# A conditioned decoder layer with expert retrieval on one core: eight first weight tiles under way, modulation rows on GpSimd's queue, top-k over two phases, gathers of u and v by turns

## The chip, the cores and the metric

One NeuronCore of a Trainium2 chip runs the whole kernel as one program. The metric is the device time of one execution in microseconds (us). The engines work in parallel, each through its own instruction list: PE (TensorE, matmul), DVE (VectorE), ACT (ScalarE), POOL (GpSimd) and SP (SyncE, which here only issues transfers). They wait for each other through semaphores. Transfers run on 16 DMA engines whoever issues them.

## The reference, cut to what matters

A prompt of 1024 tokens and 8 decoding streams of 4 tokens (32 tokens, "sample") go through one layer. All data are float32, the model width D is 1024.

```python
mod = silu(c) @ w_ada + b_ada                 # 6 rows: sh1, sc1, gt1, sh2, sc2, gt2
h1 = rmsnorm(x, g_norm1) * (1 + sc1) + sh1
mix = token_mixer(h1, ...)                    # w_in, causal pooling, conv of width 31, LayerNorm, w_out
x = x + gt1 * mix
h2 = rmsnorm(x, g_norm2) * (1 + sc2) + sh2
# PEER: 8 heads, 128 x 128 = 16384 experts, 16 chosen per head: 128 experts for each token
s = (h2 @ w_query) . sub_keys                 # two score rows of 128 for each head
sv, si = top_k(s, 16); fv, fpos = top_k(sums of the 16 x 16 pairs, 16); gate = softmax(fv)
a = u_table[eid] . h2;  act = gelu(a) * gate;  out = sum over the 128 experts of act * v_table[eid]
y = rmsnorm(x + gt2 * out, g_final)
```

Each token so reads 128 rows of 4 KB from `u_table` and 128 from `v_table`: some 1.1 GB in all.

## The kernel before, in words

**Blocks and phases.** The tokens are 8 blocks of 128 (b = 0..7) and the sample block SB = 8. Retrieval runs in phases p = 0..8 of 32 slots each. In slot c of phase p the kernel gathers u rows for block p and v rows for block p-1, four gathers each (CH = 4); one gather is an indirect DMA, issued by POOL, which brings 128 rows of 4 KB (512 KB). Phase 0 has only u, phase 8 only v and the sample block. The gathers land in two rings of six places each (`u_ring`, `v_ring`). `u_fetch` waits until DVE has freed the place six gathers back, `v_fetch` until PE has. POOL runs both in one instruction list, so whatever it waits for holds all gathers behind it.

**DVE in a slot** (`chunk`, L1324): four dots, one for each u gather (multiply by h2, sum over 1024 elements), and then the steps that `lay_out` has put into the slot before (DVE_LAG = 1). **PE in a slot** (`tokens`, L1687): the weighted sum of the v rows, and then the steps of the slot.

**Steps.** `lay_out` writes the order by hand-set costs. `fill` lays the mixer and the queries of the block groups [2,3,4] and [5,6,7,SB] from slot `at` on. `spread` lays the top-k pieces: each block has 4 parts (two heads each), each part 6 pieces (`piece`, i = 0..5), and behind them `exp` (the softmax's exponential on ACT), `nrm` (its normalisation on DVE, which waits for ACT's `exp`) and, once for a block, `turn` (the transposed expert numbers for the v gathers). The u gathers of part q of block b, at slot 32b + 8q, wait for that part's numbers. ACT runs the steps in slot order too, with a gelu after every eighth chunk, which waits for DVE's dots of that chunk.

**The head.** Before phase 0 the kernel computes the modulation (`modulation(n)`, n = 0..11, each from two tiles of `w_ada` of 1 MB; PE, then DVE adds the bias, L1089), then the mixer of blocks 0 and 1 (`project` L1509, `convolve` L1526, `taps` L1177, `pool_out`, `mean` L1556, `variance`, `mix` L1579 and L1581) and their queries and scores (L1605, L1621; ACT copies the scores out at L912). Weight tiles come through four places of 1 MB (`places`, PLACE = i % 4): tile i is issued on SP's queue once tile i-4 is used. SP also stores the modulation results to DRAM (`mod_store`), reads them back as rows broadcast to all 128 partitions (`mod_row` L535, for gt1, S2 and A2) and loads the output bias (`bout_load` L571), all in line with the tiles. The convolution's first PE_CONV channel groups run on PE with diagonal matrices that ACT makes (L819), the others as 31 taps on DVE. At the end DVE does the six pieces of part 0 of block 0, and the phases begin. After the last tile of the head SP loads x of blocks 2 and 3 (`xr_load`, L567), which DVE's step `xn` waits for.

## Time and profile before

| | |
|---|---|
| time, median of 3 runs | 3471.78 us (3471.12 to 3472.04) |
| the profiled execution | 3469.63 us, its span 3467.7 us |
| mean granted clock of TensorE | 0.82 of full speed |
| instructions in the profile | 30586 |
| busy: PE, DVE, ACT, POOL | 64%, 61%, 10%, 66% of the span |
| moved by DMA | 1253.56 MB, mean 361 GB/s |

Times below are counted from the start of the span. A row of instructions gives start and duration; in square brackets stands how long its engine was idle before it, and which instruction or transfer ended that. "issue" is time in which nothing that the profile shows was waited for. Several instructions of one kind in a row are merged and counted (x60). The phases of the retrieval begin with a dot of DVE: phase 0 at 238 us, phase 1 at 628, then 1023, 1383, 1800, 2164, 2506, 2847 and 3189.

### The profile page before, as it was taken

Reading aid. Unit: us, or ns where it says so; the run is one execution under the profiler, and the core shown is the slowest. Engines: PE = TensorE matmul, PEld = TensorE weight load, DVE = VectorE, ACT = ScalarE, POOL = GpSimd, SP = SyncE. Lnnn points to the kernel's source line nnn. Section 1 sums busy time; section 2 is a strip of 40 time slices with the busy share of each in tenths; the row PEclk is TensorE's granted clock in tenths of the full one; section 3 lists DMA queues with packets and bytes.
Section 4 is the critical chain, followed back from the end, with each engine's and each line's share of the span. In section 5 each row is a group of like instructions: output and inputs, shape, how many; then the busy total and the mean of one; then the engine's idle time right before and its main releaser. Section 6 shows DMA issues by size and latency. Waiting matters only on the chain.

```text
span 3467.7 us, 30586 instructions
## 1 busy us (share of the span) xinstructions
PE 2206.3 (64%) x9781; PEld 976.0 (28%) x9781; DVE 2125.2 (61%) x4835; ACT 360.6 (10%) x778; POOL 2283.7 (66%) x2213
## 2 busy tenths in 40 slices
PE   7873895467847899656448777454445444454576
PEld 6563452135512355211114444111111111111111
DVE  2345888645686677675655666667766776776301
ACT  3101141000111022100000010000000000000000
POOL 0012545676777777777757777777777777777675
PEclk9996897689978999888768999767777777776799
DMA  7666756899999999999989999999999999999998
GB/s 238 187 234 212 274 194 242 324 403 405 407 385 403 407 398 406 361 402 398 370 289 404 407 408 408 390 409 406 402 393 406 401 406 394 403 407 374 382 392 330
DMA packets 377968, 1253.56 MB, mean 361 GB/s; under 512 B 38056, under 2 KB 46912, under 8 KB 377793
## 3 DMA queue, kind: packets, MB, share of 16 engines
q0 software_dynamic: 304128, 1107.43, 82.3%
q1 hardware_dynamic: 51505, 100.14, 8.6%
q10 hardware_dynamic: 22176, 44.04, 3.4%
q8 instruction: 78, 1.28, 0.2%
q14 instruction: 81, 0.66, 0.0%
HBM read 1230.01 MB, written 22.06 MB: 361 GB/s over the span
## 4 chain that ended last, share of the span: by engine, by line
POOL 29%; DMA 27%; PE 24%; issue 10%; DVE 5%; SPq 3%; ACT 1%; DVEq 1%; POOLq 0%; ACTq 0%
DMA v_ring<-in_v_table_dram,eidt 21%; POOL u_ring L772 14%; POOL v_ring L789 13%; PE bank L1687 11%; PE bank L1526 4%; PE bank L1509 3%; SPq L535 2%; PE bank L1605 2%; DMA u_ring<-in_u_table_dram,eid 2%; DVE u_ring L1324 2%; DMA u_ring<-in_v_table_dram,eidt 1%; POOL u_ring L789 1%; DMA wring<-in_w_ada_dram 1%; PE bank L1581 1%; PE bank L1466 0%
## 5 line engine op out<-in xcount | busy, mean ns | idle before, releaser
L1687 PE MATMUL bank<-v_ring,act_x 128*32 128x512 f32 x3984 | 1184.2, 809 | 960.5 <-DMA v_ring<-in_v_table_dram,eidt 950.8
L1324 DVE CUSTOM_DVE_ANT_0 u_ring<-u_ring,h 128x1024 f32<-128x1024 f32 x1056 | 1281.8, 1226 | 785.4 <-DMA u_ring<-in_u_table_dram,eid 715.1
L772 POOL DMA_INDIRECT u_ring<-in_u_table_dram,eid x1024 | 1149.7, 1123 | 728.6 <-issue 299.8
L789 POOL DMA_INDIRECT v_ring<-in_v_table_dram,eidt x996 | 1036.0, 1040 | 396.4 <-issue 239.5
L1687 PEld LDWEIGHTS bank<-v_ring,act_x 128*32 128x32 f32 x3984 | 271.0, 135 | 1797.2 <-issue 1781.8
L1605 PE MATMUL bank<-hbuf,wring 128*128 128x128 f32 (+1 forms) x2048 | 243.8, 279 | 3.4 <-DMA wring<-in_w_query_dram 3.4
L1605 PEld LDWEIGHTS bank<-hbuf,wring 128*128 128x128 f32 x2048 | 236.4, 194 | 32.1 <-issue 28.4
L1526 PE MATMUL bank<-zc,dring 128*128 128x384 f32 (+1 forms) x512 | 194.4, 507 | 9.3 <-ACT dring L819 9.3
L1509 PE MATMUL bank<-hbuf,wring 128*128 128x384 f32 (+2 forms) x512 | 165.8, 483 | 23.4 <-ACT hbuf L832 22.5
L1509 PEld LDWEIGHTS bank<-hbuf,wring 128*128 128x128 f32 x512 | 99.0, 196 | 91.6 <-issue 64.0
L1581 PE MATMUL bank<-wring,mixt 128*128 128x512 f32 (+1 forms) x256 | 121.9, 627 | 0.0
L1347 DVE TENSOR_TENSOR scratch<-bank,mod 128x512 f32<-128x512 f32 x18 | 11.6, 687 | 179.2 <-PE bank L1687 177.9
L1526 PEld LDWEIGHTS bank<-zc,dring 128*128 128x128 f32 x512 | 87.8, 192 | 58.0 <-issue 26.1
L819 ACT ACTIVATE dring<-ident,cw 128x128 f32<-128x128 f32 x256 | 81.3, 393 | 123.5 <-PE bank L1528 88.2
L927 ACT ACTIVATE dot<-dot 128x32 f32<-128x32 f32 x33 | 7.6, 231 | 809.8 <-DVE dot L1324 788.2
L1324 DVE DVE_READ_ACCUMULATOR2_ANT dot<- 128x1 f32 x1056 | 87.5, 83 | 0.0
L1687 PE MATMUL bank<-u_ring,act_x 128*32 128x512 f32 x240 | 59.2, 611 | 22.5 <-DMA u_ring<-in_v_table_dram,eidt 22.5
L789 POOL DMA_INDIRECT u_ring<-in_v_table_dram,eidt x60 | 56.4, 940 | 21.7 <-issue 16.1
L1581 PEld LDWEIGHTS bank<-wring,mixt 128*128 128x128 f32 (+1 forms) x256 | 46.6, 189 | 74.9 <-issue 74.8
L902 ACT ACTIVATE qt<-bank 128x512 f32<-128x512 f32 (+1 forms) x36 | 20.2, 562 | 378.3 <-PE bank L1605 378.3
L1528 PEld LDWEIGHTS bank<-zcs,dring 128*128 128x128 f32 x248 | 46.9, 189 | 33.1
L1250 DVE TENSOR_TENSOR work<-fhalff,iota 128x512 f32<-128x512 f32 x72 | 49.8, 692 | 8.0 <-issue 0.9
(217 smaller groups left out, 1613.5 us busy)
## 6 DMA issues: line engine op xcount, KB each, us to landing
u_ring<-in_u_table_dram,eid POOLq DMA_INDIRECT x1024, 7.4
wring<-in_w_out_dram ACTq DMA_DIRECT2D x16, 1024.0 KB, 11.9
wring<-in_w_query_dram ACTq DMA_DIRECT2D x16, 1024.0 KB, 12.2
v_ring<-in_v_table_dram,eidt POOLq DMA_INDIRECT x996, 7.7
wring<-in_w_ada_dram SPq DMA_DIRECT2D x12, 1024.0 KB, 10.5
v_ring<-in_w_ada_dram SPq DMA_DIRECT2D x12, 1024.0 KB, 6.7
wring<-in_w_in_dram ACTq DMA_DIRECT2D x10, 1024.0 KB, 11.6
xr<-in_x_prompt_dram SPq DMA_DIRECT2D x16, 512.0 KB, 7.7
```

Of the source, the lines that this page charges most:

```text
L535: sp.dma_start(out.rearrange("p (n j c) -> p n j c", n=2, j=4), src.unsqueeze(0).broadcast_to([count, 2, 4, P])).then_inc(ready, 16)
L772: pool.indirect_dma_start(u_ring[:, n % NU], None, u_table[0], bass.IndirectOffsetOnAxis(ap=col, axis=0)).then_inc(u_in[n % NU], 16)
L789: pool.indirect_dma_start(place, None, v_table[0], bass.IndirectOffsetOnAxis(ap=eidt[:, b % RING, t:t + 1], axis=0)).then_inc(landed, 16)
L819: last = act.activation(diag_at(g, c, j), ident[:, :], ACT.Copy, scale=cw[:, j, c:c + 1])
L1250: dve.tensor_tensor(hot[:, :, :, :], fhalff[:, :, a * K:(a + 1) * K].unsqueeze(3).broadcast_to(shape), iota[:, :].unsqueeze(1).unsqueeze(1 ...
L1324: dve.tensor_tensor_reduce(u_ring[:, n % NU], u_ring[:, n % NU], h2[:, b % 2], 1.0, 0.0, ALU.mult, ALU.add, dot[:, b % 2, k:k + 1]).then_i ...
L1509: last = pe.matmul(ps[PROJ[c]][:, 0:n], w[:, k, c * P:(c + 1) * P], h1t[:, h * HK + k, 0:n], start=(h + k == 0), stop=(h * HK + k == KC - 1))
L1526: last = pe.matmul(ps[2 + c % 2][:, 0:np], diag_at(g, c, j), zc[:, c, j:j + np], start=(j == 0), stop=(j == CK - 1))
L1528: last = pe.matmul(ps[7][:, c * S:(c + 1) * S], diag_at(g, c, j), zcs[:, c, :, j:j + TS], start=(j == 0), stop=(j == CK - 1))
L1581: last = pe.matmul(bank, mixt[:, h * HK + k, t0:t0 + n], w[:, k, :], start=False, stop=(h * HK + k == KC - 1))
L1605: last = pe.matmul(q_bank(b)[:, a * n:(a + 1) * n], w[:, k, a * P:(a + 1) * P], h2_cols(b)[:, h * HK + k, :], start=(h + a + k == 0), stop ...
L1687: last = pe.matmul(acc[h][j * S:(j + 1) * S, :], act_x[:, i % 2, j, a:a + S], v_place(n)[0][:, h * HALF:(h + 1) * HALF], start=(c == 0), s ...
```

## The change

It has five parts.

1. **First tiles.** Tiles 0 to 7 get eight places of their own (three in `u_ring`, one more in `v_ring`); from tile 8 on four places are used as before. The load of the sub-keys, which shares memory with tile 7, waits for all eight (`mod_ps` 8). ACT makes its first eight diagonals after x's columns instead of before them.
2. **Modulation rows.** The stores of modulation results 4 to 9, the broadcast rows of gt1, S2 and A2 and the first load of the output bias are issued by POOL, which waits for each result in turn; 10 and 11 stay on SP. Semaphores of the sample's rows are separate now. PE and DVE do modulations 4 to 9 in one run behind the convolution (PE), and behind taps and boxes (DVE); PE's `pool_out` comes after them.
3. **Convolution split.** PE_CONV goes from 2 to 1: one channel group on PE, three as taps on DVE.
4. **Steps.** `exp` and `nrm` of part 0 of block 0 move from slot 0 to slot 5, the mixer of the second group begins at slot 5 instead of 2, block 0's parts 1 to 3 are spread over slots 0 to 18, and block b's four parts over slots 18 + 30(b-1) to 18 + 30b (block 1 was within slots 13 to 31, block b from 8 slots after its predecessor's phase began to 5 slots after its end).
5. **Gathers.** POOL issues u, v, u, v, ... instead of four u and four v.

```diff
-PLACE = [i % 4 if i < FIRST else (i - FIRST) % 2 for i in range(len(TILES))]
+PLACE = [i if i < 8 else i % 4 if i < FIRST else (i - FIRST) % 2 for i in range(len(TILES))]
...
-    at = 2
+    at = 5
...
-    first = [("exp", 0, 0), ("nrm", 0, 0)] + top_steps([(part, 0) for part in range(1, PARTS)] + [(part, 1) for part in range(PARTS)])
-    spread(first, 0, NCH)
-    for b in range(2, NB):
-        spread(top_steps([(part, b) for part in range(PARTS)]), (b - 1) * NCH + 8, b * NCH + 5)
-    spread(top_steps([(part, SB) for part in range(PARTS)]), LAST * NCH + 6, NB * NCH - 3)
+    spread(top_steps([(part, 0) for part in range(1, PARTS)]), 0, 18)
+    slots[5] += [("exp", 0, 0), ("nrm", 0, 0)]
+    for b in range(1, NB):
+        spread(top_steps([(part, b) for part in range(PARTS)]), 18 + 30 * (b - 1), 18 + 30 * b)
+    spread(top_steps([(part, SB) for part in range(PARTS)]), 18 + 30 * LAST, NB * NCH - 3)
...
-        PE_CONV = 2
+        PE_CONV = 1
...
+            pool.wait_ge(proj_ps, projected_at(0, 2, G - 1))
+            pool.dma_start(bout, b_out).then_inc(bout0_in, 16)
+            for n in range(4, 10):
+                pool.wait_ge(mod_taken, n + 1)
+                pool.dma_start(mod_dram[n], modst[:, n % 2]).then_inc(mod_stored[n % 2], 16)
+                if n % 2:
+                    for i in range(2):
+                        pool.wait_ge(mod_stored[i], 16 * (n // 2 - 1))
+                    out, ready = {5: (gt1[:, :], gt1_in), 7: (mod2[:, S2], mod2_in), 9: (mod2[:, A2], mod2_in)}[n]
+                    mod_row(pool, out, n // 2, 0, P, ready)
...
                     for j in range(CH):
                         if p < NB or c < NSG:
                             u_fetch(p, c * CH + j)
-                    for j in range(CH):
                         if p:
                             v_fetch(p - 1, c * CH + j)
...
             act.wait_ge(par_ready, 1)
             ahead = [(c, q) for c in range(PE_CONV) for q in range(NQ)]
-            for c, q in ahead[:2]:
-                diagonals(0, c, q)
             act.wait_ge(modt_ready, 1)
             for b in GROUPS[0]:
                 x_columns(b)
+            for c, q in ahead[:2]:
+                diagonals(0, c, q)
...
             taps(PE_CONV, G)
-            modulation(4)
-            modulation(5)
             boxes(0)
-            modulation(6)
-            modulation(7)
             dve.wait_ge(g2_in, 16 * 4)
-            modulation(8)
-            modulation(9)
+            for n in range(4, 10):
+                modulation(n)
             centre(0)
...
-            convolve(0, 0, 0, NQ)
-            modulation(4)
-            modulation(5)
-            convolve(0, 1, 0, NQ)
-            modulation(6)
-            modulation(7)
+            for c in range(PE_CONV):
+                convolve(0, c, 0, NQ)
+            keys_turned(0)
+            keys_turned(1)
+            for n in range(4, 10):
+                modulation(n)
             for c in range(G):
                 pool_out(0, c)
-            modulation(8)
-            modulation(9)
-            keys_turned(0)
-            keys_turned(1)
             mean(0)
```

## Rows read from the trace of the kernel before

**Rows 1.** The page: busy time of the engines, and the chain by engine.

```profile
PE 2206.3 (64%) x9781; PEld 976.0 (28%) x9781; DVE 2125.2 (61%) x4835; ACT 360.6 (10%) x778; POOL 2283.7 (66%) x2213
POOL 29%; DMA 27%; PE 24%; issue 10%; DVE 5%; SPq 3%; ACT 1%; DVEq 1%; POOLq 0%; ACTq 0%
```

**Rows 2.** Windows by phase: busy PE, PEld, DVE, ACT, POOL; clock, DMA share, GB/s.

```profile
238.00:628.00 390.00, 247.12 (x957) 154.16 (x955) 297.00 (x749) 91.29 (x212) 180.34 (x133) 0.82 0.71 240
628.00:1023.00 395.00, 268.17 (x1466) 143.78 (x1466) 234.76 (x506) 38.99 (x73) 278.74 (x255) 0.85 1.01 394
1023.00:1383.00 360.00, 309.66 (x1221) 143.02 (x1218) 248.33 (x573) 66.86 (x178) 273.06 (x256) 0.93 1.02 401
1383.00:1800.00 417.00, 233.41 (x743) 68.79 (x739) 262.97 (x564) 32.50 (x52) 294.46 (x257) 0.78 0.96 362
1800.00:2164.00 364.00, 284.17 (x1722) 165.51 (x1722) 229.70 (x506) 28.44 (x50) 275.03 (x257) 0.89 1.03 407
2506.00:2847.00 341.00, 166.91 (x516) 39.02 (x514) 234.27 (x530) 12.34 (x21) 262.30 (x257) 0.74 1.02 402
```

**Rows 3.** Timeline, 254 to 290 us; columns: start, duration, instruction, idle time before.

```profile
254.97 1.22 DVE L1324 CUSTOM_DVE_ANT_0 u_ring<-u_ring,h 128x1024 f32<-128x1024 f32 x1 [0.81 <-DMA u_ring<-in_u_table_dram,eid]
...
288.52 1.43 SPq L567 DMA_DIRECT2D xr<-in_x_prompt_dram  x2
288.89 0.23 ACT L917 ACTIVATE gate<-gate 128x32 f32<-128x32 f32 x1
289.15 0.19 DVE L1297 TENSOR_REDUCE fsum<-gate 128x2 f32<-128x32 f32 x1 [32.95 <-ACT gate L917]
```

**Rows 4.** Timeline of DVE: first and last instruction of one part of top-k.

```profile
211.71 0.29 DVE L1229 MAX8 sv<-v_ring 128x8 f32<-128x128 f32 x1 [8.24 <-ACT v_ring L912]
231.31 0.18 DVE L1291 CAST eid<-eidf 128x32 uint32<-128x32 f32 x1
```

**Rows 5.** Waits, then lines of DVE, 296 to 628 us; busy us, mean ns, idle.

```profile
DVE u_ring L1324 <- DMA u_ring<-in_u_table_dram,eid: 6.7, 6, 2.5
DVE mixt L1186 <- PE bank L1556: 4.9, 1, 4.9
...
L1324 DVE CUSTOM_DVE_ANT_0 u_ring<-u_ring,h 128x1024 f32<-128x1024 f32 x120 | 140.4, 1222 | 10.0 <-DMA u_ring<-in_u_table_dram,eid 6.7 <-issue 1.0
```

**Rows 6.** Timeline of ACT and PE in phase 0.

```profile
355.62 0.23 ACT L927 ACTIVATE dot<-dot 128x32 f32<-128x32 f32 x1 [10.46 <-DVE dot L1324]
...
359.56 51.53 PE L1509 MATMUL bank<-hbuf,wring 128*128 128x384 f32 x151
427.06 20.24 PE L1526 MATMUL bank<-zc,dring 128*128 128x384 f32 x62 [1.93 <-ACT dring L819]
522.77 2.82 PE L1556 MATMUL bank<-mixt,mean_w 128*128 128x384 f32 x8 [0.76 <-ACT mixt L865]
```

**Rows 7.** Timeline of the head, 74 to 194 us.

```profile
74.69 28.59 DVE L1177 SCALAR_TENSOR_TENSOR mixt<-zc,cw,mixt 128x256 f32<-128x256 f32 x60
121.44 1.23 SPq L526 DMA_DIRECT2D wring<-in_w_ada_dram  x2
134.99 1.94 PE L1466 MATMUL bank<-wring,y 128*32 128x128 f32 x32 [2.22 <-DMA wring<-in_w_ada_dram]
152.90 2.04 PE L1579 MATMUL bank<-hbuf,ones 1*128 1x512 f32 x2 [7.47 <-DMA hbuf<-in_b_out_dram]
...
193.23 0.16 DVE L1221 RECIPROCAL nst<-nst 128x1 f32<-128x1 f32 x1 [16.52 <-DMA mod<-mod_scratch]
```

**Rows 8.** Lines of POOL, 2506 to 2847 us, then timeline at 2629 us.

```profile
L789 POOL DMA_INDIRECT v_ring<-in_v_table_dram,eidt x129 | 132.5, 1027 | 40.0 <-issue 32.9 <-PE bank L1687 7.1
L772 POOL DMA_INDIRECT u_ring<-in_u_table_dram,eid x128 | 130.3, 1018 | 39.0 <-issue 39.0
...
2629.63 1.23 DVE L1324 CUSTOM_DVE_ANT_0 u_ring<-u_ring,h 128x1024 f32<-128x1024 f32 x1 [1.01 <-DMA u_ring<-in_u_table_dram,eid]
2629.73 1.93 POOL L772 DMA_INDIRECT u_ring<-in_u_table_dram,eid  x1 [0.30 <-issue]
```

More of the change, by code:

```diff
@@ L308, in build @@
         modst = y[:, KC * S:KC * S + 2 * P].rearrange("p (n c) -> p n c", n=2)
+        more += [r[:, a:a + 2, :].rearrange("p a (b n) -> p (a b) n", n=HALF) for r, a in ((u_ring, 0), (u_ring, 2), (u_ring, 4), (v_ring, 4))]
         places = [wring[:, 0], wring[:, 1]] + more
@@ L349, in build @@
             sem(n) for n in ("c_in", "par_in", "wp_in", "key_in", "bada_in", "g2_in", "gfin_in"))
-        w_at = [sem(f"w_at{i}") for i in range(4)]
+        w_at = [sem(f"w_at{i}") for i in range(8)]
         xr_in = [sem(f"xr_in{i}") for i in range(2)]
-        bout_in, gt1_in, mod2_in, gt2_in, h2_in, y_in = (
-            sem(n) for n in ("bout_in", "gt1_in", "mod2_in", "gt2_in", "h2_in", "y_in"))
+        bout0_in, gt1_in, mod2_in = (sem(n) for n in ("bout0_in", "gt1_in", "mod2_in"))
+        bout_in, gt1s_in, mod2s_in, gt2_in, h2_in, y_in = (
+            sem(n) for n in ("bout_in", "gt1s_in", "mod2s_in", "gt2_in", "h2_in", "y_in"))
         u_in = [sem(f"u_in{i}") for i in range(NU)]
@@ L509, in v_place, with mod_row @@
             return u_ring[:, k - NV], u_in[k - NV], U_ALL // NU + m
+        def mod_row(eng, out, n, r, count, ready):
+            src = mod_dram[2 * n:2 * n + 2].rearrange("n (j q) c -> q n j c", q=S)[r]
+            eng.dma_start(out.rearrange("p (n j c) -> p n j c", n=2, j=4), src.unsqueeze(0).broadcast_to([count, 2, 4, P])).then_inc(ready, 16)
         def xr_at(*use):
@@ L526, in tile @@
                 sp.dma_start(places[PLACE[i]], tile_source(i)).then_inc(w_at[PLACE[i]], 16)
-            def mod_store(n):
-                sp.wait_ge(mod_taken, n + 1)
-                sp.dma_start(mod_dram[n], modst[:, n % 2]).then_inc(mod_stored[n % 2], 16)
-            def mod_row(out, n, r, count, ready):
-                src = mod_dram[2 * n:2 * n + 2].rearrange("n (j q) c -> q n j c", q=S)[r]
-                sp.dma_start(out.rearrange("p (n j c) -> p n j c", n=2, j=4), src.unsqueeze(0).broadcast_to([count, 2, 4, P])).then_inc(ready, 16)
-            def mod_wait(n):
-                for i in range(2):
-                    sp.wait_ge(mod_stored[i], 16 * (n - 1))
             def xr_load(i):
@@ L656, in _ @@
                 was = TILES[i - 4]
-                if was[0] == "ada" and was[1] >= 4 and was[2]:
-                    mod_store(was[1])
                 if was[0] == "q" and was[3]:
@@ L681, in _ @@
                     xr_load(3)
+                elif i == TILE_NO["q", 0, 0, 1]:
+                    sp.dma_start(gfin[:, :], g_final.rearrange("(a d) -> a d", a=1).broadcast_to([P, D])).then_inc(gfin_in, 16)
                 elif i == TILE_NO["q", 0, 2, 1]:
+                    for n in (10, 11):
+                        sp.wait_ge(mod_taken, n + 1)
+                        sp.dma_start(mod_dram[n], modst[:, n % 2]).then_inc(mod_last, 16)
                     x1_store(0)
@@ L685, in _ @@
             spill(PARTS - 1, 1)
[L686 to L687 removed]
+            sp.wait_ge(mod_last, 16 * 2)
+            mod_row(sp, mod2[:, GT2], 5, 0, P, gt2_in)
             xr_load(4)
@@ L982, in _ @@
                 if m == 0:
-                    while batch_freed(0, *ahead[made]) == 0:
+                    while made < len(ahead) and batch_freed(0, *ahead[made]) == 0:
                         diagonals(0, *ahead[made])
@@ L1199, in add_x @@
                 dve.wait_ge(mix_ps, b + 1)
-                dve.wait_ge(gt1_in, 16 if b < NB else 16 * (1 + NS))
+                if b < NB:
+                    dve.wait_ge(gt1_in, 16)
+                else:
+                    dve.wait_ge(gt1s_in, 16 * NS)
                 xr_wait(dve, "x1", b)
@@ L1215, in norm @@
                     dve.tensor_tensor_reduce(scratch[:, :], x, x, 1.0, 0.0, ALU.mult, ALU.add, nst[:, b % 2, 0:1]).then_inc(ss_done, 1)
-                dve.wait_ge(mod2_in, 16 * (2 if b < NB else 2 + 4 * NS * 2))
+                if b < NB:
+                    dve.wait_ge(mod2_in, 16 * 2)
+                else:
+                    dve.wait_ge(mod2s_in, 16 * 4 * NS * 2)
                 if 2 <= b < NB:
@@ L1572, in mix @@
                 if first and b == GROUPS[g][0]:
-                    pe.wait_ge(bout_in, 16 * (g + 1))
+                    if g:
+                        pe.wait_ge(bout_in, 16 * g)
+                    else:
+                        pe.wait_ge(bout0_in, 16)
                     pe.wait_ge(cm_ready, g + 1)
```

21 lines of the change are left out of this document (5 added, 16 removed).

## The prediction

> **What bounds the kernel now.** I read the page first. No engine is busy for more than two thirds of the span, and the chain that ended last is POOL 29%, DMA 27%, PE 24% [rows 1]: the bound changes with the stage, so I cut the span at the first dot of each phase. Windows by phase [rows 2] show three regimes. The head takes 238 us. Phase 0 takes 390 us at 240 GB/s while DVE is busy for 297 of them. From 628 us on the DMA share is 1.01 to 1.03 and the rate 394 to 407 GB/s, but for the phase from 1383 us (0.96; DVE waits there for the sample's rows, which this change leaves on SP). The three quiet phases (2164, 2506 and 2847 us; one row stands for them) take 341 us each at 402 GB/s.
>
> In phase 0 the waits of DVE tell two stories. At its start DVE stands still for 32.95 us [rows 3]: it waits for ACT's exponential of part 0, which ACT, in its own order, makes only after the last score copy of the head. Behind 296 us it waits little: 6.7 us for gathers and 4.9 us for the mean [rows 5]. So phase 0 is set by DVE's work, 120 dots and seven parts of top-k. The quiet phases are set by two things that nearly tie. POOL needs 132.5 + 130.3 us for 257 gathers and 79 us between them [rows 8], together 341.8, which is the whole phase; and DMA moves 402 GB/s, where the best phase reaches 407 [rows 2], by which the same bytes would take 337 us.
>
> **Phase 0: the stall.** With `exp` and `nrm` at slot 5, DVE meets `nrm` at chunk 6. What it needs before that is part 1's scores, which PE and ACT make well before the head's last ones. From 256.2 us on, DVE does chunks 2 to 5 and their pieces in the time that it now waits: one part of top-k is 231.5 - 211.7 = 19.8 us [rows 4], a dot 140.4/120 = 1.17 us and 1.25 with what lies between [rows 5]. Up to the end of chunk 6 that is 20 dots (25 us) and five pieces of six (17 us): 256.2 + 42 = 298 us. ACT's exponential is there at 289.1, and the x tiles are issued at 288.5 [rows 3], so neither should hold it. Before, DVE was at chunk 3 at that time; now it is at 6. That is worth the whole 33 us.
>
> **Phase 0: top-k moved out.** Before, 41 pieces lie in slots 0 to 30, after it 18 (block 0) and 11 (block 1, every 1.25 slots from slot 18): 12 fewer, two parts, 2 x 19.8 = 39.6 us. DVE's own sum thus ends 72.6 us sooner. Starting the group 3 slots later also moves its two residual additions into the next phase, some 8 us.
>
> **Phase 0: PE is late next.** The mixer of the second group is a chain on PE, 163 us from `project` (359.56) to the mean (522.77) [rows 6]. It began at 359 because ACT had a gelu before x's columns in slot 7, released by the dots of chunk 7 (355.62) [rows 6]. In slot 10 the columns come well behind that gelu; what they wait for is x of block 4, normalised at chunk 8. From 298: 5 us for the first two x tiles, then two chunks and their pieces at 8.3 us each, 2.5 us for the third x, 5 us for transposes and columns: 326 to 328. The mean then comes at 328 + 163 + 3 = 494 us. DVE is at chunk 25 by about 467 and waits 27 us, where it now waits 4.9: this is the new wait. From there it has 24 dots (30 us), five pieces (16 us) and centring, scaling and one normalisation (8 us) to the end of the phase. Phase 1 begins at about 550 instead of 628. I take **-77 us**. The ends: -108 if nothing waited (33 + 39.6 + 8 and the 27 of the wait), which the PE chain forbids, and -45 if PE's `project` started no earlier than at 350. The same top-k work falls into phase 1, where DVE is busy for 235 of 395 us [rows 2]: 12 pieces more (40 us) leave it 120 us of slack, hidden by the transfers.
>
> **Bytes moved.** About 1.5 to 2 MB of stores and weight tiles leave phase 0, which has room, for phases that are full at 0.4 MB/us: **+4 us** (0 to 8).
>
> **The head.** Eight tiles under way: DMA is saturated from the first microseconds until tile 7 has landed, so their order is unchanged, -2 to 0. Taps: a tap is 28.59/60 = 0.477 us [rows 7], and 31 more are 14.8 us; DVE is through at 118 instead of 103 and, with the boxes, takes modulation 4 at 122. PE loses one convolution (14 us) and waits for that. The tiles of modulations 8 and 9 are issued when 6 and 7 are used, the last of them at 126.4 instead of 121.4 [rows 7], so modulation 9 ends 5 us later than before (134.99 + 1.94 = 137 [rows 7]); pool_out (4 us) now follows it, and the mean is 8 us late. But PE's `mix` now waits 1.5 us for the bias, loaded late in SP's line (152.90 [rows 7]); it would start at 159. Then the other side: DVE waited 16.52 us for S2 and A2 until 193.23 [rows 7]. POOL issues these rows now. No row shows POOL issuing 1024 pieces of 512 B; SP's issue of such a row takes 0.4 us, a gather of 128 pieces takes POOL 0.94, eight times that is 7.5. I take 7.5, since POOL makes each piece itself. Three rows and six stores then end at about 160 us, the last lands by 172, and h2 of block 0 is ready right behind `mix`, at 187 instead of 196. PE takes it after `mix` of block 1, at 195: the queries start where they did, within 1 us. Sum of the head **0**; ends -5 (rows at 0.4 us each and tiles sooner) and +14 (a row costs POOL 20 us).
> The Trainium skill ("DMA: Bandwidth & Descriptors", section "Issuing engines are not separate DMA queues") says that another issuing engine saves only the time of issuing; by it the move of the rows is worth what SP's line cost, which is the same zero.
>
> **The steady phases: gathers by turns.** This is the disputed term. A gather takes 0.94 us, but one that begins inside a dot ends 0.8 us after that dot: 1.93 us at 2629.73, when a dot ran from 2629.63 to 2630.86 [rows 8]. The whole quiet phase has only 132.5 + 130.3 - 257 x 0.94 = 21 us of such excess. It is small because four u gathers land about 1.29 us apart (512 KB at 407 GB/s), so four dots (1.23 us each) form a train in which the next gather finds the gap, and a top-k piece of up to 5.1 us fits behind the train while four v gathers land. By turns a u gather lands every 2.6 us. A dot on time still meets one gather at its very end (cost under 0.1 us). But a piece of 1.9 to 5.1 us no longer fits between two dots (1.3 us): after each piece one to three dots are late, and a late dot costs POOL about half its length, 0.6 us. 24 pieces x 0.6 = 14 us in a phase, of which POOL and DMA between them can hide part, while gathers lie queued ahead of the transfers. I take +5 in each of the three quiet phases and nothing in the other four, where POOL has 16 to 39 us of slack against the transfers (395 - 279 - 77 = 39 in phase 1 [rows 2]): **+15 us**. The ends: -10 (up to 12 gathers in flight instead of 10, and fewer gaps), and +204, from full randomness: dots cover 157 of 341 us, so 46% of 256 gathers would wait 0.61 us, 72 us of excess instead of 21.
> The Trainium skill ("SBUF — State Buffer", "SBUF: two separate sides") speaks against the change here: the port pair of DVE and GpSimd is an exclusive lock, which a DVE instruction with two SBUF inputs holds to its end while the other blocks. The 1.93 us agree. By the rule alone a dot under every second gather is the worst order, and the sum would end near 3600; by the row, which shows trains that slip past each other, it stays under 3500.
>
> **Sum.** 3469.6 us (profiled execution, 2 us under the median of the runs) - 77 + 4 + 0 + 15 = 3412 us.
>
> **Rivals.**
> 1. *Alternation is free*: POOL and DMA tie as before and the lead hides the late dots. For it: landings are evenly spaced, so the lock could settle as it has. 3469.6 - 77 + 4 = 3397 us.
> 2. *The gain of phase 0 is partly eaten by PE*: `project` begins at 350, because x of block 4 or ACT's order holds it, and phase 1 at 580 or later. For it: PE is busy for 247 of the 390 us [rows 2]. 3469.6 - 48 + 4 + 15 = 3441 us.
> 3. *Slower: dots break POOL's pace*. Half of the way to randomness, 25 us more excess in a phase. It decides where POOL's time passes that of the transfers: quiet phases 257 x 1.24 + 46 = 365 instead of 341, three times +24; the phases of 360 and 364 us (273 and 275 busy + 77 + 25) +15 and +13; the other two 0. 3397 + 100 = 3497 us. The point from which it outweighs phase 0 is 18 us more of excess in a phase. Against it: the excess after pieces alone is 14.
> That the change doesn't do what it says is small here: that `nrm` no longer stands in slot 0 is plain in the order of steps.
>
> **Chances.** Forecast 50% (3412, own range 3400 to 3430), rival 1 18%, rival 2 12%, rival 3 17%, the rest 3%. The range, 3375 to 3485 us, holds all but most of rival 3. A difference of 0.2% (7 us) is what a measurement can tell: faster 0.79, same 0.04, slower 0.17.
>
> **What would show it.** Right: no wait of DVE on `gate` near 256 us; the first dot of phase 1 near 550; a wait of DVE for the mean of 20 to 30 us; queries at 199 +/- 3; quiet phases of 341 to 350 us with a mean gather of 1.03 to 1.06 us. Wrong: quiet phases over 360 us with a mean gather over 1.1 (rival 3), `project` after 345 (rival 2), or a wait of `norm` for its rows in the head.

## The result and the profile after

The changed kernel takes 3537.68 us (median of 4 runs, 3524.2 to 3546.39), the kernel before 3471.45 us beside it (3469.0 to 3472.04): ratio 1.019, 95% interval 1.016 to 1.022. It is 66 us slower where 3412 us was forecast, and 53 us over the upper end of the range. The profiled execution took 3524.2 us, its span 3522.4. It was the quickest of the four, so lengths of stages below add up to some 55 us and not to 66.

The page of the changed kernel, busy times and chain by engine ([rows 1] before): POOL has 72 us more of busy time for ten more instructions, and in the chain its share rises from 29 to 35%.

```profile
PE 2276.8 (65%) x9719; PEld 958.1 (27%) x9719; DVE 2124.4 (60%) x4866; ACT 361.3 (10%) x755; POOL 2355.3 (67%) x2223
POOL 35%; DMA 24%; PE 20%; issue 12%; DVE 5%; SPq 3%; ACT 1%; DVEq 1%; POOLq 0%; ACTq 0%
```

Windows by phase, cut at the first dots (239, 566, 969, 1348, 1770, 2144, 2508, 2868 and 3242 us), columns as in [rows 2]:

```profile
239.00:566.00 327.00, 234.68 (x924) 147.77 (x924) 255.10 (x607) 86.11 (x205) 175.79 (x131) 0.87 0.77 270
566.00:969.00 403.00, 284.62 (x1482) 147.09 (x1480) 254.64 (x575) 40.09 (x67) 285.07 (x257) 0.86 1.02 397
969.00:1348.00 379.00, 299.65 (x1143) 132.04 (x1144) 250.00 (x580) 68.23 (x178) 285.98 (x256) 0.89 0.99 380
1348.00:1770.00 422.00, 263.82 (x814) 80.68 (x813) 267.19 (x593) 37.25 (x67) 297.59 (x262) 0.79 0.97 369
1770.00:2144.00 374.00, 275.37 (x1650) 155.10 (x1650) 232.24 (x520) 28.13 (x49) 274.62 (x254) 0.88 0.98 385
2508.00:2868.00 360.00, 184.49 (x516) 36.98 (x514) 234.72 (x546) 14.88 (x23) 275.08 (x255) 0.74 0.98 380
2868.00:3242.00 374.00, 197.74 (x519) 37.94 (x515) 245.45 (x579) 15.11 (x24) 281.78 (x256) 0.67 0.96 364
```

Phase 0 is 63 us shorter (327 for 390). All that and more is lost again in the seven full phases: 2676 us from 566 to 3242, where it was 2561 (628 to 3189), so 115 us more. The three quiet phases take 364, 360 and 374 us for 341 to 343, and transfers fall from 402 to 380 and 364 GB/s with a DMA share under one: the transfers no longer set these phases. DVE's busy time there is unchanged (234.27 and 234.72 us), and TensorE's clock isn't the reason either: in the phase at 2508 us it is 0.74 as before, and the phase is 19 us longer all the same.

POOL by line in the quiet phase at 2508 us ([rows 8] before):

```profile
L790 POOL DMA_INDIRECT v_ring<-in_v_table_dram,eidt x127 | 143.3, 1129 | 46.0 <-issue 34.2 <-PE bank L1692 11.8
L773 POOL DMA_INDIRECT u_ring<-in_u_table_dram,eid x128 | 132.2, 1033 | 39.0 <-issue 39.0
```

143.3 + 132.2 + 46.0 + 39.0 = 360.5 us, the whole phase, as 341.8 was before. Busy and idle time fill any window; what points at POOL is that 73.2 of its 85.0 idle us are the 0.30 us between two gathers ("issue"), so that it hardly waits for a place. It has 12.7 us more inside gathers and 6 us more between them. A stretch of the timeline of that phase shows how:

```profile
2602.02 1.22 DVE L1330 CUSTOM_DVE_ANT_0 u_ring<-u_ring,h 128x1024 f32<-128x1024 f32 x1 [1.33 <-DMA u_ring<-in_u_table_dram,eid]
2603.04 1.01 POOL L773 DMA_INDIRECT u_ring<-in_u_table_dram,eid  x1 [0.30 <-issue]
...
2605.25 1.23 DVE L1330 CUSTOM_DVE_ANT_0 u_ring<-u_ring,h 128x1024 f32<-128x1024 f32 x1
...
2605.59 1.69 POOL L773 DMA_INDIRECT u_ring<-in_u_table_dram,eid  x1 [0.30 <-issue]
...
2607.14 1.23 DVE L1330 CUSTOM_DVE_ANT_0 u_ring<-u_ring,h 128x1024 f32<-128x1024 f32 x1 [0.65 <-DMA u_ring<-in_u_table_dram,eid]
2607.59 1.58 POOL L790 DMA_INDIRECT v_ring<-in_v_table_dram,eidt  x1 [0.31 <-issue]
...
2619.56 0.94 POOL L773 DMA_INDIRECT u_ring<-in_u_table_dram,eid  x1 [0.30 <-issue]
2619.61 1.22 DVE L1330 CUSTOM_DVE_ANT_0 u_ring<-u_ring,h 128x1024 f32<-128x1024 f32 x1
...
2620.76 1.22 DVE L1330 CUSTOM_DVE_ANT_0 u_ring<-u_ring,h 128x1024 f32<-128x1024 f32 x1
2620.80 1.98 POOL L790 DMA_INDIRECT v_ring<-in_v_table_dram,eidt  x1 [0.30 <-issue]
```

The first pair is the case that the prediction had in mind: the gather meets the last 0.2 us of a dot and takes 1.01 us instead of 0.94. Then a piece of top-k (2603.34 to 2605.2) delays a dot, the gather at 2605.59 meets most of it and takes 1.69. That gather is late by its own hold, so the next dot, which finds DVE idle again, meets the next gather too (1.58). The one after that begins ahead of a dot and takes 0.94 us, so the good order is back. At 2620 us three dots run in a row behind a longer piece; the gather that begins 0.04 us into the third takes 1.98 us.

This is the rule in the three quiet phases. Of their 762 gathers 147 take over 0.3 us more than 0.94. Behind such a gather the next one is held as long in 18% of the cases, behind any other in 19%, so in general a held gather does not make the next one held; only behind those held by a dot that followed another instruction at once is it 12 of 29, and one gather later 2 of 29. The disturbance is short and starts at the pieces: of the 114 us that these gathers take over 0.94 each, 79 lie in the 403 gathers that begin during other work of DVE than dots or up to 3.75 us behind it. In the kernel before it is 37 of 65 us, in 421 gathers, so 42 of the 49 us of increase lie there.

### The profile page after: what moved, and what is told of

The parts are those of the page before. It is cut to its first block, busy times and chain, and to the rows that moved or that the text cites. A ratio compares the mean times of both kernels' runs of the same rounds, so it can differ in the third digit from the quotient of the medians.

```text
span 3522.4 us, 30468 instructions
## 1 busy us (share of the span) xinstructions
PE 2276.8 (65%) x9719; PEld 958.1 (27%) x9719; DVE 2124.4 (60%) x4866; ACT 361.3 (10%) x755; POOL 2355.3 (67%) x2223
## 4 chain that ended last, share of the span: by engine, by line
POOL 35%; DMA 24%; PE 20%; issue 12%; DVE 5%; SPq 3%; ACT 1%; DVEq 1%; POOLq 0%; ACTq 0%
DMA v_ring<-in_v_table_dram,eidt 18%; POOL v_ring L790 17%; POOL u_ring L773 16%; PE bank L1692 8%; PE bank L1610 3%; PE bank L1528 3%; SPq L518 2%; PE bank L1586 2%; PE bank L1511 2%; DVE u_ring L1330 2%; DMA u_ring<-in_u_table_dram,eid 2%; DMA u_ring<-in_v_table_dram,eidt 1%; POOL u_ring L790 1%; DMA xr<-in_x_prompt_dram 1%; DVE mixt L1177 1%
## 5 line engine op out<-in xcount | busy, mean ns | idle before, releaser
L1692 PE MATMUL bank<-v_ring,act_x 128*32 128x512 f32 x3984 | 1262.4, 793 | 928.3 <-DMA v_ring<-in_v_table_dram,eidt 918.7
L790 POOL DMA_INDIRECT v_ring<-in_v_table_dram,eidt x996 | 1108.6, 1113 | 444.4 <-issue 268.2
L1692 PEld LDWEIGHTS bank<-v_ring,act_x 128*32 128x32 f32 x3984 | 257.4, 129 | 1825.0 <-issue 1802.2
L1528 PE MATMUL bank<-zc,dring 128*128 128x384 f32 x496 | 189.4, 508 | 8.3 <-ACT dring L819 8.3
L1692 PE MATMUL bank<-u_ring,act_x 128*32 128x512 f32 x240 | 57.3, 595 | 22.4 <-DMA u_ring<-in_v_table_dram,eidt 22.4
```

Of the source, the lines that this page charges most:

```text
L790: pool.indirect_dma_start(place, None, v_table[0], bass.IndirectOffsetOnAxis(ap=eidt[:, b % RING, t:t + 1], axis=0)).then_inc(landed, 16)
L1528: last = pe.matmul(ps[2 + c % 2][:, 0:np], diag_at(g, c, j), zc[:, c, j:j + np], start=(j == 0), stop=(j == CK - 1))
L1692: last = pe.matmul(acc[h][j * S:(j + 1) * S, :], act_x[:, i % 2, j, a:a + S], v_place(n)[0][:, h * HALF:(h + 1) * HALF], start=(c == 0), s ...
```

## The experiments

Each kernel ran beside the kernel before on the same chip. Changes are against the changed kernel unless said otherwise. Every ratio is to the kernel before as it ran beside it, with its 95% interval.

| kernel | gathers | median us | ratio |
|---|---|---|---|
| changed kernel | turns | 3537.68 | 1.019 [1.016, 1.022] |
| e2_turns_only | turns | 3573.87 | 1.028 [1.026, 1.030] |
| e1_fours | fours | 3434.42 | 0.988 [0.986, 0.989] |
| e3_steps_only | fours | 3432.01 | 0.987 [0.986, 0.989] |
| e8_head_only | fours | 3472.57 | 1.000 [0.999, 1.001] |
| e4_pairs | pairs | 3464.36 | 0.997 [0.996, 0.998] |
| e5_turns_onein | turns | 3437.85 | 0.990 [0.988, 0.992] |
| e6_fours_onein | fours | 3404.34 | 0.981 [0.979, 0.983] |
| e7_x_early | fours | 3426.76 | 0.988 [0.986, 0.990] |

The kernel before took 3471.45 us beside the changed kernel, 3474.19 beside e1, e2, e3 and e8, and 3473.66 beside e4 to e7.

**e1_fours: the turns undone.**

```diff
                             u_fetch(p, c * CH + j)
+                    for j in range(CH):
                         if p:
```

> The changed kernel with one part undone: POOL again issues four u gathers and then four v. Theory (turns cost POOL time, because dots of DVE that are not in a train hold its gathers): the 115 us that the phases from 1 to 7 gained go away, the 62 us of phase 0 stay: 3405 to 3425 us, quiet phases 341 to 345 us, mean gather there 1.02 to 1.04 us. Rival (it is the new spacing of the top-k pieces, every 1.25 slots and on into the next phase, that lengthens the phases): about 3520 us, quiet phases 360 us or more.

Measured: 3434.42 us. The turns cost 103 us; without them the change would be a gain of 40. The profiled executions differ by 87 us: 92 in the seven full phases and 3 behind them, less 9 in phase 0, where nothing goes by turns.

**e2_turns_only: the same edit alone, on the kernel before.** The `for` line between `u_fetch` and `v_fetch` is taken out of the kernel before, nothing else.

> The kernel before with turns alone (u, v, u, v). Theory: phases 1 to 7 grow by 100 to 130 us and nothing is gained in phase 0: 3560 to 3600 us, mean gather of the quiet phases 1.08 to 1.11 us. Rival (spacing of top-k): 3465 to 3480 us, since top-k stays where it was.

Measured: 3573.87 us, 100 us over its own kernel before. So the loss does not hang on the new order of steps.

**e3_steps_only: part 4 of the change alone, on the kernel before.**

```diff
-    at = 2
+    at = 5
...
-    first = [("exp", 0, 0), ("nrm", 0, 0)] + top_steps(...)
+    spread(top_steps([(part, 0) for part in range(1, PARTS)]), 0, 18)
+    slots[5] += [("exp", 0, 0), ("nrm", 0, 0)]
```

> The kernel before with the new order of steps alone (top-k over two phases, exp and nrm at slot 5, mixer from slot 5). Theory: phase 0 falls from 390 us to 325 to 335, the later phases stay within 10 us in all: 3405 to 3425 us. Rival (spacing of top-k costs the later phases 115 us): about 3520 us.

(The diff is shortened: the lines for the later blocks are those of part 4.) Measured: 3432.01 us, 42 us gained, but 7 us over the upper end of what was expected, as e1_fours is 9 us over it. The two agree within the intervals, so the steps are the whole gain. Phase 0 takes 333 us instead of 390, but the seven full phases give back 29 us (2590 for 2561); in e1_fours they give back 23 (2584 for 2561).

**e8_head_only: parts 1 to 3 (first tiles, POOL's rows, PE_CONV = 1), with the old steps and gathers in fours.**

```diff
-    at = 5
+    at = 2
...
+                    for j in range(CH):
                         if p:
```

> The kernel before with the head's parts alone (eight first tiles, modulation rows on POOL, one channel group on PE); steps and gathers as before. Both theories: no change, 3465 to 3480 us, first dot at 236 to 241 us.

(Shortened too: the old `spread` lines come back as well.) Measured: 3472.57 us, ratio 0.9996 [0.9986, 1.0005]: nothing, as forecast. The profiled execution had its first dot at 244.1 us, though, where 236 to 241 was expected.

**e4_pairs: u, u, v, v.**

```diff
-                    for j in range(CH):
-                        if p < NB or c < NSG:
-                            u_fetch(p, c * CH + j)
-                        if p:
-                            v_fetch(p - 1, c * CH + j)
+                    for j0 in range(0, CH, 2):
+                        for j in (j0, j0 + 1):
+                            if p < NB or c < NSG:
+                                u_fetch(p, c * CH + j)
+                        for j in (j0, j0 + 1):
+                            if p:
+                                v_fetch(p - 1, c * CH + j)
```

> The changed kernel with its gathers in twos: u, u, v, v. Theory (a gather that begins inside a dot is held to the dot's end; trains of dots slip past the gathers, pieces of top-k break short trains): between fours and turns, 3460 to 3510 us, mean gather of the quiet phases between 1.03 and 1.09 us. Rival (only strict alternation of the two tables' reads hurts, whatever the dots do): as the fours, 3425 to 3445 us. Second rival (any other order than four and four hurts equally): 3530 to 3550 us.

Measured: 3464.36 us, 30 us over fours and 73 under turns. POOL by line in its quiet phase at 2478 us (353 us long):

```profile
L773 POOL DMA_INDIRECT u_ring<-in_u_table_dram,eid x127 | 136.7, 1076 | 38.7 <-issue 38.7
L790 POOL DMA_INDIRECT v_ring<-in_v_table_dram,eidt x128 | 132.9, 1038 | 45.0 <-issue 31.7 <-PE bank L1694 13.3
```

The mean gather is (136.7 + 132.9) / 255 = 1.057 us, between the 1.018 of fours and the 1.080 of turns. The shorter the train of dots, the more the gathers are held.

**e5_turns_onein and e6_fours_onein: the same gathers, dots that do not hold them.** Both replace the dot by a sum over the u row, in turns and in fours. Left out is the product with h2, so the v rows get other weights; experts, bytes and order stay.

```diff
-                    dve.tensor_tensor_reduce(u_ring[:, n % NU], u_ring[:, n % NU], h2[:, b % 2], 1.0, 0.0, ALU.mult, ALU.add,
-                                             dot[:, b % 2, k:k + 1]).then_inc(u_free, 1)
+                    dve.tensor_reduce(dot[:, b % 2, k:k + 1], u_ring[:, n % NU], AX, ALU.add).then_inc(u_free, 1)
```

> The changed kernel (u, v by turns), with each dot replaced by a sum over the u row alone: the same length of work, but only one operand in SBUF besides the result; left out is the product with h2, so the weights of the v rows are other numbers. Theory (a dot with two SBUF operands holds the gather's issue): the mean gather falls from 1.08 to 1.10 us in the quiet phases to 0.94 to 0.97, and the quiet phases to what the transfers need, 335 to 343 us each; 3395 to 3430 us in all, equal within 10 us to the same kernel with fours. Rival (the order in which the rows land, the rings or the DMA queues cost the 100 us): still 3520 to 3545 us.

> Gathers four and four with the new steps and the new head, each dot replaced by a sum over the u row alone (left out is the product with h2). Theory: nothing holds a gather, mean 0.94 to 0.97 us, and the transfers set every full phase: 3395 to 3430 us, a little under 3434. Rival (the excess of the gathers is not the dots'): 3430 to 3440 us, with a mean gather of 1.02 to 1.03 us in the quiet phases as before.

Measured: 3437.85 us by turns, 3404.34 in fours. A timeline of e5_turns_onein, the same kind of stretch as above:

```profile
2599.61 1.22 DVE L1330 TENSOR_REDUCE dot<-u_ring 128x1 f32<-128x1024 f32 x1 [1.95 <-DMA u_ring<-in_u_table_dram,eid]
2600.35 0.94 POOL L790 DMA_INDIRECT v_ring<-in_v_table_dram,eidt  x1 [0.30 <-issue]
...
2604.41 2.34 DVE L1330 TENSOR_REDUCE dot<-u_ring 128x1 f32<-128x1024 f32 x2
2604.63 0.94 POOL L790 DMA_INDIRECT v_ring<-in_v_table_dram,eidt  x1 [2.10 <-PE bank L1691]
2605.87 0.94 POOL L773 DMA_INDIRECT u_ring<-in_u_table_dram,eid  x1 [0.30 <-DVE dot L1330]
```

The instruction on DVE is as long as the dot (1.22 us), but three gathers begin inside one and take 0.94 us each. In the whole trace 798 gathers begin with over 0.15 us of a sum left, and none takes longer than 0.95.

The edit changes more than the number of operands: the dot also writes its 1024 products back to `u_ring`, the sum writes one number. The trace of the changed kernel separates the two:

```profile
374.53 0.69 DVE L1259 TENSOR_TENSOR work<-work,sif 128x512 f32<-128x512 f32 x1
374.78 1.25 POOL L773 DMA_INDIRECT u_ring<-in_u_table_dram,eid  x1 [0.30 <-issue]
...
587.89 1.29 DVE L1206 TENSOR_TENSOR scratch<-bank,gt 128x512 f32<-128x512 f32 x2 [0.20 <-issue]
588.92 0.94 POOL L773 DMA_INDIRECT u_ring<-in_u_table_dram,eid  x1 [0.31 <-issue]
...
1433.80 2.75 DVE L1191 RECIPROCAL hbuf<-hbuf 128x416 f32<-128x416 f32 x1
1434.82 0.94 POOL L773 DMA_INDIRECT u_ring<-in_u_table_dram,eid  x1 [0.30 <-issue]
```

A product of two SBUF operands holds the gather (1.25 us). The same instruction with one operand in PSUM (`bank`) doesn't, nor does a reciprocal with one operand, though both write their full width to SBUF. So what the instruction reads decides here, not what it writes. One full-width operand is not always harmless: a TENSOR_SCALAR of 1024 columns, done in 0.76 us from 337.91 on, holds the gather of 338.42 for 1.06 us. POOL by line in a quiet phase, first of e1_fours (2471 to 2815 us), then of e5_turns_onein (2476 to 2823), then of e6_fours_onein (2442 to 2783):

```profile
L790 POOL DMA_INDIRECT v_ring<-in_v_table_dram,eidt x129 | 131.6, 1020 | 45.0 <-issue 29.6 <-PE bank L1693 15.4
L773 POOL DMA_INDIRECT u_ring<-in_u_table_dram,eid x128 | 130.0, 1016 | 39.0 <-issue 39.0
```

```profile
L790 POOL DMA_INDIRECT v_ring<-in_v_table_dram,eidt x129 | 123.0, 954 | 64.0 <-PE bank L1691 34.1 <-issue 29.9
L773 POOL DMA_INDIRECT u_ring<-in_u_table_dram,eid x129 | 121.6, 942 | 39.3 <-issue 32.9 <-DVE dot L1330 6.1 <-PE bank L1691 0.3
```

```profile
L773 POOL DMA_INDIRECT u_ring<-in_u_table_dram,eid x128 | 122.2, 955 | 39.0 <-issue 22.9 <-DVE dot L1331 16.2
L790 POOL DMA_INDIRECT v_ring<-in_v_table_dram,eidt x128 | 121.4, 949 | 57.8 <-PE bank L1692 31.8 <-issue 25.9
```

With one operand POOL waits for free places (31.8 and 34.1 us for PE's), which is how it looks when it is ahead of the transfers. The four kernels make a square: the hold costs 3434 - 3404 = 30 us in fours and 3538 - 3438 = 100 us by turns. So of the 103 us of the turns the hold by dots carries 70, and some 34 stay when no dot holds a gather. Half of what e5_turns_onein was expected to show came: the gathers fell to 0.95 us as the theory said, but the time stayed 34 us over fours and 8 us over the upper end of 3395 to 3430.

The seven full phases of the two traces differ by these 34 us (2594 for 2560). Windows of both in the last of them, the first five slots and the rest, show where part of it lies. e5_turns_onein, then e6_fours_onein:

```profile
2823.00:2886.00 63.00, 25.75 (x84) 5.98 (x81) 43.10 (x71) 5.06 (x8) 37.55 (x40) 0.69 0.86 335
2886.00:3173.00 287.00, 149.03 (x437) 30.68 (x434) 199.38 (x381) 10.05 (x16) 200.55 (x212) 0.80 1.00 396
```

```profile
2783.00:2840.00 57.00, 27.01 (x83) 6.13 (x81) 42.40 (x70) 5.06 (x8) 38.59 (x40) 0.65 0.96 378
2840.00:3124.00 284.00, 145.34 (x442) 33.36 (x437) 203.45 (x381) 10.05 (x16) 202.38 (x214) 0.72 1.01 402
```

Two thirds of the difference lie in the first five slots. There POOL stands for a place in the v ring, 13.5 us at a stretch in the one and 6.1 in the other: PE can't take the first v row of a block before the block's last dots and its weights.

**e7_x_early: SP loads x of blocks 2 and 3 sooner (against e1_fours).**

```diff
                     x1_store(1)
+                    xr_load(4)
+                    xr_load(5)
             spill(PARTS - 1, 1)
...
             mod_row(sp, mod2[:, GT2], 5, 0, P, gt2_in)
-            xr_load(4)
-            xr_load(5)
```

> Gathers four and four, new steps and head, and SP issues the x tiles of blocks 2 and 3 right behind the stores of x1 (at about 236 us) instead of behind the last spills, the GT2 row and a full queue (288 us). Theory (the 21.7 us wait of DVE for x in phase 0 is a real loss): phase 0 shortens by 18 to 22 us, of which a few come back later: 3410 to 3420 us. Rival (PE's chain to the mean sets the end of phase 0, so the wait for the mean grows from 12 us to 30): 3428 to 3436 us.

Measured: 3426.76 us, ratio 0.9878 [0.9858, 0.9899]; 0.9877 had e1_fours. The wait for x, 21.7 us in e1_fours, is gone; the wait for the mean is 12.6 us (12.4 in e1_fours), so the rival's long wait for the mean did not come. Instead the waits for u gathers grew from 22.4 to 32.8 us, which is why only part of the 21.7 is gained. These are all of DVE's waits that come to over 2 us in phase 0 (236 to 558 us), with the total, how often, and the longest:

```profile
DVE u_ring L1331 <- DMA u_ring<-in_u_table_dram,eid: 32.8, 21, 7.3
DVE mixt L1187 <- PE bank L1559: 12.6, 1, 12.6
DVE eidt L1314 <- PE bank L1641: 6.9, 1, 6.9
```

Phase 0 is 322 us long for 336, and the profiled execution's span 18 us shorter, but the medians differ by 8 and the intervals can't tell the two kernels apart. It has the lowest median of the working kernels at the usual rate of transfers, and beats both kernels of this case; over e1_fours and e3_steps_only no gain is shown.

**Ten runs with slow transfers.** Later the kernel before took 3664.4 us (beside e9 to e12), 3662.0 (beside e12b, e7b, e9b and e11b) and 3636.34 (beside after_again and e1b): in the quiet phases of all ten kernels the transfers moved some 360 to 370 GB/s, where the fours had moved some 400. Only comparisons within such a group are used.

| kernel | median us | ratio |
|---|---|---|
| e9_weigh_early | 3600.37 | 0.981 [0.978, 0.985] |
| e10_mixer_slot4 | 3608.87 | 0.985 [0.981, 0.989] |
| e11_both | 3594.84 | 0.978 [0.975, 0.982] |
| e12_turns_weigh_early | 3643.56 | 0.994 [0.992, 0.996] |
| e7b_x_early | 3590.39 | 0.980 [0.974, 0.987] |
| e9b_weigh_early | 3601.67 | 0.981 [0.974, 0.987] |
| e11b_both | 3595.81 | 0.982 [0.976, 0.988] |
| e12b_turns_weigh_early | 3642.57 | 0.994 [0.992, 0.997] |
| after_again | 3625.44 | 0.996 [0.994, 0.998] |
| e1b_fours | 3584.81 | 0.985 [0.982, 0.987] |

e9 makes a block's weights ahead of the next phase's first dots, e10 begins the mixer one slot sooner, e11 has both, all on e7_x_early; e12 is the changed kernel with the edit of e9. Labels with a b are the same kernels again. The edit of e9, then that of e10:

```diff
+                    if p and c == 0:
+                        weigh(p - 1)
                     if p < NB or c < NSG:
                         chunk(p, c)
...
-                    if p and c == 0:
-                        weigh(p - 1)
```

```diff
-    at = 5
+    at = 4
```

> e7_x_early with one step moved: DVE makes the weights of the block just ended before the first four dots of the next phase, not behind them and the slot's pieces. Theory of the phase boundary (PE can take no v row of the block until its weights are there, the v ring fills and POOL stands, 5 to 9 us a phase; DMA share 0.96 to 0.98 in the first 58 us of a phase against 1.01 later): that stall goes, each of the seven full phases gains 1 to 3 us: 3407 to 3420 us against 3427. Rival (the transfers owe this time anyway, later in the phase): 3422 to 3430 us.

> e7_x_early with the mixer of the second group from slot 4 on instead of 5. Theory (PE's chain to the mean sets phase 0, and each slot of delay pushes work of the last group into phases 5 and 6): 3418 to 3425 us, of which some 5 us in phase 0. Rival (DVE waits one slot earlier for x of block 4, which PE's transposes release only behind the head's last scores): a new wait of 5 to 10 us for x, 3427 to 3435 us.

> Weights early and the mixer from slot 4 on, on top of e7_x_early. If both are real they add: 3400 to 3415 us. If neither is: 3422 to 3435 us.

> The changed kernel, by turns, with the weights made before the first dots of a phase. Theory: of the 100 us that the turns cost, the first five slots of each phase carry 17 us in the three quiet phases (66 us instead of 60), because by turns the last u of a block lands as late as its last v while the v of the next are already queued; that part goes, 20 to 40 us in seven phases: 3500 to 3520 us. The rest, gathers held by dots, stays: mean gather of the quiet phases still 1.08 to 1.10 us. Rival (the boundary is only where the held gathers show first): 3530 to 3540 us.

> The changed kernel by turns with the weights made before the first dots of a phase, again, beside a kernel before that moves its usual 400 GB/s (in the call before it took 3664 us and moved 360 to 370). Theory of the boundary: 3500 to 3520 us, 20 to 40 us under the changed kernel's 3538, with a mean gather of the quiet phases still 1.08 to 1.10 us. Rival (the boundary is only where held gathers show first): 3530 to 3540 us.

> Gathers four and four, x tiles early, again as the partner of the two that follow: 3420 to 3430 us where the kernel before takes 3474.

> e7_x_early with the weights before the first dots, again. Where transfers were slow it came to 0.981 of the kernel before, against 0.988 for e7_x_early at the usual rate. Theory: the stall of the v ring at the start of each phase goes, 3405 to 3420 us. Rival (transfers owe the time anyway): equal to e7b_x_early within 5 us.

The forecasts in microseconds can't be judged, since they stood on 400 GB/s. By ratio, neither edit shows anything: e9b equals its partner e7b (0.981 and 0.980), e11 and e11b (0.978 and 0.982) have intervals that overlap with those of e9, e9b and e7b, and e10 has no partner in its group without the edit. By turns, e12 and e12b (0.994) and the changed kernel (0.996) can't be told apart either, and in the quiet phase from 2950 us of e12b POOL still stands 8.4 us for a place in the v ring, where after_again stands 8.8:

```profile
POOL v_ring L790 <- PE bank L1692: 8.4, 1, 8.4
```

So making the weights sooner didn't take the stall away, and the theory of the phase's start is not shown. What releases PE there was not tried further.

The last group has the turns beside the fours at slow transfers:

> The changed kernel itself, as the partner of e12b. If transfers are slow again (kernel before near 3662): theory (held gathers cost only where GpSimd's pace passes that of the transfers) says that turns cost much less than 100 us, as the transfers need 370 us in a quiet phase and GpSimd 355 to 365: 3640 to 3665 us, ratio 0.995 to 1.001; the boundary theory adds that it is slower than e12b's ratio of 0.994 by 0.003 or more. Rival (turns cost their 100 us whatever the transfers do): ratio 1.015 to 1.02. If transfers are back at 400 GB/s: 1.019 as before.

> The changed kernel with gathers four and four, as the partner of after_again. With slow transfers: theory 0.980 to 0.984 of the kernel before (the gain of the steps, 40 us, and some of it more because DMA is the only bound), so turns cost 45 to 70 us between the two. With transfers back at 400 GB/s: 0.988.

Measured: 3625.44 and 3584.81 us, so the turns cost 41 us here and 103 at the usual rate; the changed kernel is even a little faster than the kernel before (0.996). Windows of the quiet phase, after_again (2558 to 2936 us), then e1b_fours (2556 to 2926 us):

```profile
2558.00:2936.00 378.00, 193.25 (x516) 37.99 (x514) 234.76 (x546) 14.89 (x23) 280.24 (x257) 0.69 0.96 362
```

```profile
2556.00:2926.00 370.00, 178.84 (x520) 38.94 (x516) 236.95 (x545) 14.90 (x23) 266.65 (x257) 0.69 0.98 370
```

The mean gather by turns is 280.24 / 257 = 1.09 us, held as much as before, but the fours now need 370 us for their transfers and not 344. The fours are also held more than before: over the three quiet phases gathers take 93 us over 0.94 each, for 61 at the usual rate, and by turns 127 for 114. So the turns add 34 us of hold here and 53 there; the phases grew by 15 us here and by 60 there (the profiled executions differ by 23 us here, not by 41). Most of the fall from 60 to 15 is thus cover by the transfers and some of it is less hold. That held gathers cost little where the transfers are slower than POOL anyway was the theory's claim; the 41 us lie just under its 45 to 70 and far from the rival's fixed 100.

## Why the prediction was wrong

**The mechanism forecast as a rival at 17% is what happened** (rival 3, "dots break POOL's pace", 3497 us; measured 3538). The 3412 us failed by 112 us against the profiled execution (3524.2). By its own terms:

- *The steady phases, +15 us.* This is the step that failed. Against e1_fours the turns cost 92 us in the seven full phases (2676 for 2584) and 103 in the medians. The term had two parts, the excess ("24 pieces x 0.6 = 14 us in a phase") and its cover ("of which POOL and DMA between them can hide part"; +5 in each quiet phase "and nothing in the other four"). The excess came out near its size, though not on the dots that were named. Counted over the three quiet phases of the changed kernel and of the kernel before (excess is a gather's duration over 0.94 us, and a dot is late if it begins right behind another instruction), gathers have 114 us of excess for 65, so 17 us more in a phase. Late dots are 88 of 384 for some 50 (28 to 68, by the gap that still counts as "right behind"), and gathers that began inside them cost 26.0 us for 6.4: 6.5 us a phase more and not 14. Gathers that began inside dots on time cost 82.1 us for 49.6: 260 of them at 0.32 us each, where "under 0.1" was put. (The fours before had 0.17 there.) The sentence "a dot on time still meets one gather at its very end" holds on the undisturbed beat; in the few us behind a piece it doesn't, as at 2607 us, and most of the increase lies there.
- *The cover* was the larger mistake: there was none. POOL had next to no waits in a quiet phase to give up (7.1 us in [rows 8]), so each microsecond of hold came out at its end, and POOL's idle time beyond 0.30 us before a gather grew as well, from 11 to 36 us in the three. 49 + 25 = 74 us, and the three phases are 73 us longer. Part of that is the new steps: against e1_fours hold and waits grow by 53 and 12 us, and the phases by 60. Nor did the slack of the other phases hide it: against e1_fours phases 1 to 4 are 3, 12, 8 and 9 us longer.
- *The range of that term, -10 to +204,* held the result. Rival 3 took 25 us more excess in a phase and 100 us in all; 17 us in a phase came with 103. By the square of four kernels, some 34 of the 103 us stay even when no dot holds a gather; no case of the prediction had such a loss, and its cause stays open. Two of the prediction's figures don't follow from its rows: by rival 3's own sum the gain of phase 0 is used up at 20 us of excess a phase and not 18, and full randomness gives some +245 us and not +204. Neither moves the forecast.
- The Trainium skill ("SBUF — State Buffer", "SBUF: two separate sides") said that a DVE instruction with two SBUF inputs locks the port pair that it shares with a GpSimd instruction that reads SBUF, for its whole length. The pair of kernels with one operand agrees: same length on DVE, gathers at 0.94 instead of up to 1.98 us. The page lets whichever starts first block the other, and that is not so in this trace: the dot of 2619.61 begins 0.05 us behind a gather and takes 1.22 us as ever, and of 819 dots that begin inside a gather none takes over 1.26. The prediction put the page aside for the row of trains; the page's direction was right, and the prediction's "near 3600" was 62 us too far.
- *Phase 0, -77 us.* Measured -63 in the changed kernel. The stall of 33 us at `nrm` is gone and no wait for `gate` is in the trace. What failed is "the x tiles are issued at 288.5, so neither should hold it". They were issued when forecast, behind two 1 MB tiles, two spills and a row, but the issue of the two alone took 9.49 us and they were there only at 315.9:

```profile
288.85 9.49 SPq L563 DMA_DIRECT2D xr<-in_x_prompt_dram  x2
...
315.93 1.23 DVE L1099 CUSTOM_DVE_ANT_0 scratch<-xr 128x1024 f32<-128x1024 f32 x1 [17.60 <-DMA xr<-in_x_prompt_dram]
```

  `project` began at 344.90 (forecast 328), the mean's matmul at 507.69 (about 494), phase 1 at 566 (550). The wait for the mean was 12.5 us and not 20 to 30, since DVE had already lost 17.6. e7_x_early takes the cause away and its phase 0 is 14 us shorter than that of e1_fours.
- *Bytes, +4 us.* The new steps cost the seven full phases 23 us in e1_fours and 29 in e3_steps_only. In e1_fours phases 1 and 2 are 4 and 8 us longer than before, so the top-k work that moved there was not wholly hidden by the transfers. Another 8 lie in phase 5 (350.6 for 343 us), to which the mixer's three slots of delay move the last scores of the last group (slot 162 instead of 159; phase 5 begins at 160). This cause is argued, not tried: e10_mixer_slot4 ran only with slow transfers.
- *The head, 0.* Right in size: the first dot comes at 239.28 us (238 before), e8_head_only is at 1.000, and the queries begin at 201.5 (199 ± 3). A single trace says little here, since the first dot of kernels with the new head came anywhere from 236.0 (e7_x_early) to 250.4 us (e5_turns_onein); why is not known. The price of a broadcast row on POOL was wrong and didn't matter: 0.90 us, where 7.5 was taken and 0.4 was the lower end.

## What to carry to other kernels

Where two engines' instructions exclude each other, the order of many small ones is a resource: read the mean duration of the blocked instruction by phase against its shortest one, and ask of a new order whether it keeps what makes them slip past each other after a disturbance, not just on the undisturbed beat. Count every blocked instruction in the few us behind a disturbance, not only the first; and where the blocked engine has no waits to give up, nothing hides the hold. And a load that is issued when it was issued before does not land when it landed before, if what it waits behind has moved.

## What the runs showed of the hardware

- A gather issued by GpSimd is held by a dot with two SBUF operands until about 0.8 us after the dot's end (2605.59 + 1.69 = 2607.28, dot's end 2606.48), and not at all by a sum of the same 1.22 us with one SBUF operand. For this kernel that is 30 us even in the best order: 3404 us with everything in place but the product with h2.
- A row of 512 KB broadcast from DRAM costs POOL 0.90 us of issue and a 64 KB store 0.55, whatever its many pieces; a gather of 128 rows costs 0.94. In the head of the changed kernel:

```profile
125.74 1.09 POOL L756 DMA_DIRECT2D mod_scratch<-y  x2
139.19 0.90 POOL L518 DMA_DIRECT2D mod<-mod_scratch  x1 [12.36 <-DMA mod_scratch<-y]
```

- The rate of the gathers is no constant: gathers in fours moved 398 GB/s in a quiet phase of e1_fours and 370 in the same kernel later (e1b_fours), and the kernel before took 3471 to 3474 us and later 3636 to 3664. One and the same chip showed both. What an order of issue costs changed with it from 103 to 41 us.
